# Other costs and a tiling charge in the list scheduler of a six-layer transformer kernel

## What is computed

```python
for i in range(DEPTH):                      # 4 layers, kinds 0, 1, 2, 0
    ...                                     # x @ w_in, rope on q and k
    mix = dsa_attention / dilated_attention / moba_attention
    mo = memory_attention(qm, mk, mv)       # 4 heads over 256 memory rows
    x = layer_norm(ALPHA * x + concat(mix, mo) @ w_out[i])
    x = layer_norm(ALPHA * x + swiglu(x, w_gate_up[i], w_down[i]))
for l in range(DEPTH_2):                    # 2 layers
    ...                                     # h = rms_norm(x), u = h @ w_in[l]
    oa = diff_attention(...)                # 4 heads, two maps each
    ob = mla_attention(...)                 # 8 heads of width 64 + 32
    oc = sliding_window_attention(...)      # 8 heads with sinks
    y = gates0 * (oa @ w_br_a) + gates1 * (ob @ w_br_b) + gates2 * (oc @ w_br_c)
    x = x + rms_norm(y @ w_out)
    x = x + sigmoid(x @ w_ple_gate) * (p @ w_ple_proj)
```

## Time and profile before

| | |
|---|---|
| median of 3 runs | 1916.89 us (1916.48 to 1917.0) |
| profiled execution, its time | 1914.78 us |
| profiled execution, its span | 1912.9 us |
| TensorE busy | 1866.8 us, 98% |
| GpSimd busy | 1520.1 us, 79% |
| ScalarE busy | 938.1 us, 49% |
| VectorE busy | 813.0 us, 42% |

### The profile page before, as it was taken

One profiled execution on the slowest core, in us unless ns is written; L12 is line 12 of the kernel. 1 busy time (PEld: TensorE's weight loads), 2 busy tenths in 40 slices (PEclk: granted clock), 3 DMA queues, 4 the chain that ended last, 5 costly groups with the idle time before them and its releaser, 6 DMA issues.

```text
span 1912.9 us, 27394 instructions
## 1 busy us (share of the span) xinstructions
PE 1866.8 (98%) x9610; PEld 1528.5 (80%) x9610; DVE 813.0 (42%) x1944; ACT 938.1 (49%) x1485; POOL 1520.1 (79%) x1330
## 2 busy tenths in 40 slices
PE   7999999999999999999999999999999999999998
PEld 6778888877888887788888678887787887788877
DVE  7884110446311155411147741106747445446534
ACT  4554444454544345444435644434656644555752
POOL 7758989885897977797987679797786887777785
PEclk9999999999999999999999999999999999999999
DMA  8444656564776554465655446655564564556453
GB/s 285 127 151 152 189 153 234 182 190 111 202 199 209 183 180 149 140 187 154 234 157 153 162 157 186 196 191 169 174 181 129 156 203 162 163 175 178 131 168 107
DMA packets 184557, 330.54 MB, mean 173 GB/s; under 512 B 12220, under 2 KB 44520, under 8 KB 184424
## 3 DMA queue, kind: packets, MB, share of 16 engines
q1 hardware_dynamic: 176512, 323.21, 54.6%
q10 hardware_dynamic: 7912, 5.59, 1.0%
HBM read 325.35 MB, written 3.41 MB: 172 GB/s over the span
## 4 chain that ended last, share of the span: by engine, by line
PE 85%; DVE 6%; POOL 5%; DMA 1%; issue 1%; ACT 1%; ACTq 0%; DVEq 0%
PE acc L1412 24%; PE acc L1413 23%; PE acc L1419 21%; POOL w_lo L1182 5%; PE tps L1359 4%; PE acc L1434 3%; PE acc L1415 2%; PE ops L1476 2%; PE tps L1452 2%; DMA raw<-in_w_down 1%; PE acc L1383 1%; PE acc L1385 1%; PE acc L1384 1%; PE ops L1371 1%; DMA L<-in_positions 0%
## 5 line engine op out<-in xcount | busy, mean ns | idle before, releaser
L1182 POOL TENSOR_TENSOR w_lo<-raw,w_hi 128x512 fp32r<-128x512 f32 (+2 forms) x1242 | 1479.2, 1228 | 346.8 <-ACT w_hi L1210 345.7
L1210 ACT CAST w_hi<-raw 128x1024 fp32r<-128x1024 f32 (+3 forms) x624 | 615.5, 992 | 746.7 <-PE acc L1419 567.4
L1412 PE MATMUL acc<-w_hi,xT_hi 128*128 128x512 f32 (+1 forms) x1808 | 687.4, 384 | 13.5 <-POOL w_lo L1182 3.6
L1413 PE MATMUL acc<-w_lo,xT_hi 128*128 128x512 f32 (+1 forms) x1808 | 666.4, 372 | 0.0
L1419 PE MATMUL acc<-w_hi,xT_lo 128*128 128x512 f32 (+2 forms) x1744 | 505.1, 371 | 0.5 <-DVE xT_lo L1689 0.5
L1412 PEld LDWEIGHTS acc<-w_hi,xT_hi 128*128 128x128 f32 x1808 | 341.3, 189 | 86.6 <-issue 22.2
L1413 PEld LDWEIGHTS acc<-w_lo,xT_hi 128*128 128x128 f32 x1808 | 342.1, 189 | 51.9
L1419 PEld LDWEIGHTS acc<-w_hi,xT_lo 128*128 128x128 f32 x1744 | 317.6, 189 | 58.6 <-DVE xT_lo L1689 1.6
L1749 DVE TENSOR_TENSOR H<-G,acc 128x512 f32<-128x512 f32 (+1 forms) x48 | 30.9, 644 | 334.5 <-PE acc L1419 334.5
L1412 PE MATMUL acc<-w_hi,hT_hi 128*128 128x512 f32 x352 | 139.6, 397 | 2.9 <-POOL w_lo L1182 2.5
L1413 PE MATMUL acc<-w_lo,hT_hi 128*128 128x512 f32 x352 | 137.3, 390 | 0.0
(11 more groups left out here) (208 smaller groups left out, 2000.7 us busy)
## 6 DMA issues: line engine op xcount, KB each, us to landing
raw<-in_w_gate_up SPq DMA_DIRECT2D x160, 512.0 KB, 3.8
raw<-in_w_in SPq DMA_DIRECT2D x104, 512.0 KB, 3.9
raw<-in_w_down SPq DMA_DIRECT2D x88, 512.0 KB, 3.9
raw<-in_w_out SPq DMA_DIRECT2D x48, 512.0 KB, 3.5
raw<-in_w_in_a SPq DMA_DIRECT2D x32, 512.0 KB, 3.8
raw<-in_w_in_b SPq DMA_DIRECT2D x20, 512.0 KB, 4.6
raw<-in_w_mem_kv SPq DMA_DIRECT2D x16, 512.0 KB, 4.2
raw<-in_w_gate_up SPq DMA_DIRECT2D x32, 256.0 KB, 2.8
```

Of the source, the lines that this page charges most:

```text
L1182: ins = nc.gpsimd.tensor_tensor(w_lo[:, r, i, 0:ch.width], raw[:, r, i, 0:ch.width], w_hi[:, slot, i, 0:ch.width].bitcast(F32), ALU.subtract)
L1210: nc.scalar.copy(w_hi[:, u.u % SPLIT, 0:u.nk, 0:u.chunk.width], raw[:, u.u % RAW, 0:u.nk, 0:u.chunk.width]).then_inc(S["hi_ready"], 1)
L1412: nc.tensor.matmul(o, hi[:, tok], wh, start=first_k, stop=False)
L1413: ins = nc.tensor.matmul(o, hi[:, tok], wl, start=False, stop=False)
```

## The change

The list scheduler gets a notion of tiling. Scores, values and index tasks count as tiled, all other tasks of TensorE do not. If TensorE's last task was tiled, any task that isn't can begin only 250 ns (LEAVE) after its clock; a tiled task that follows another kind ends 90 ns later (ENTER). The cost of scores goes from 450 ns for each map to 100 + 0.33 for each column of all maps, that of values from 800 to 350 ns. The code that emits instructions is not changed; their order and the PSUM banks that tasks get come from the list.

```diff
--- before.py
+++ after.py
@@ -47,6 +47,7 @@
 SPLIT = 8
 LAG = 5
 CROSS = 120
+ENTER, LEAVE = 90, 250
 FIRST_CONSTANTS = 3
 CONSTANTS = 8
 REL_CONSTANTS = 3
@@ -341,12 +342,19 @@
                     best = (at, slots)
             return best
 
+        def tiled(k):
+
+            return k.kind in ("scores", "values", "index")
+
+        mode = False
         left = len(self.tasks)
         while left:
             first = None
             for e, tasks in ready.items():
                 for k in tasks:
                     at = max(k.at, clock[e])
+                    if e == "PE" and mode and not tiled(k):
+                        at = max(at, clock[e] + LEAVE)
                     if k.room is not None:
                         where = place(k)
                         if where is None:
@@ -366,7 +374,11 @@
                     rooms[k.room[0]][b] = k
             k.begin = first[0][0]
             k.end = k.begin + k.cost
+            if k.eng == "PE" and tiled(k) and not mode:
+                k.end += ENTER
             clock[k.eng] = k.end
+            if k.eng == "PE":
+                mode = tiled(k)
             if k.sem is not None:
                 count[k.sem] = count.get(k.sem, 0) + k.inc
                 k.n = count[k.sem]
@@ -500,7 +512,7 @@
             s.qk = qk[i] if isinstance(qk, dict) else qk
             b1, b3 = s.before, s.before3
             wide = s.width * s.maps
-            s.scores = self.task("PE", "scores", s, 450 * s.maps, "scores_ready",
+            s.scores = self.task("PE", "scores", s, 100 + 0.33 * wide, "scores_ready",
                                  [*s.qk, *s.apart, b1.scores if i else None], prio=0,
                                  room=("acc", s.banks or score_banks))
             after = [s.scores, s.mask_at]
@@ -529,7 +541,7 @@
                 s.take[j] = self.task("DVE", "take_turn", (s, j), 160 + 1.03 * P * blocks, "t_taken",
                                       [s.turn[j], b1.values if b1 is not None else None], prio=0)
                 s.turn[j].release = s.take[j]
-            s.values = self.task("PE", "values", s, 800, "pv_ready", [*s.take[:s.turns], *s.fed], prio=0,
+            s.values = self.task("PE", "values", s, 350, "pv_ready", [*s.take[:s.turns], *s.fed], prio=0,
                                  room=("ops", [(0,), (1,)]))
             if s.flipped:
                 ready = s.values
```

## The result

The changed kernel takes 1925.15 us (median of 7 runs, 1921.67 to 1931.78), the kernel before beside it 1917.0 us (1914.58 to 1918.95). The ratio is 1.0041, with a 95% interval of 1.0026 to 1.0055: slower by some 8 us. Lines of the code stand 12 further down: products are L1424, L1425, L1427 and L1431, scores L1446, transposes of probabilities L1464, values L1488.

A forecast was written before the change was run, and what follows sets the result against it. TensorE was taken as the bound. From the profiled 1914.78 us, merges took 1.2, wrongly tiled tasks and waits 0, giving 1913.6; the median lies 2.1 higher, so 1915.7 us, with an 8-in-10 range of 1905 to 1926.

The forecast's parts named there:

- The bound and where to look: TensorE sets the end; only the six stretches with attention, idle 22.4 us together, can change much.
- The merges: Tiled tasks becoming neighbours in TensorE's order: four at 0.14 us and three at 0.21, together 1.2 us saved.
- The wait term: All TensorE waits together, moved by the new order: taken as 0, bounds -8.5 and +10 us.
- the thin cover: End of layer 3's attention: no next layer's memory products there; TensorE waits 1.11 us for VectorE's low part.
- The rival of the late chain: Planner's clock runs short, splits and evictions queue, uncovered tails end later: 1920.7 or 1925.7 us; chance 0.25.
- Fewer waits: Rival: short costs put more products between scores and transposes, so the softmax is ready: about 1909 us; chance 0.35.
- The wrong set of tiled tasks: Latent scores and differential values, 8 + 8 tasks, charged as tiled although they are not: 0, bound 4 us.
- What moves with it: Transposes behind scores come 0.8 us later, with VectorE's copy, values, ScalarE's output and w_out products; costs nothing where covered.
- The clock: TensorE's granted clock in the stretches, read as 0.99 or 1.00 of full speed; no term for it.
- The feed-forward stretches: They hold no tiled task; a difference there would contradict the whole picture.

The follow-up runs named there:

- lengths in layer 3 alone: The changed kernel with measured lengths of scores and values for layer 3's steps only, other stretches keeping their order: 1920.34 us, 1.0023 to before.
- measured lengths: The changed kernel with scores and values costs as the rows give them: 1917.85 us; with latent scores and differential values also not counted as tiled, 1915.42 us.

## Why the prediction failed, step by step

**The bound and where to look: right.** TensorE sets the end, and the six stretches are 8.5 us longer where the whole span grew by 8.9 (the start gives 1.7 back, the feed-forward stretches take 2.0); 6.3 us of them are idle time, beyond the 4 us that the prediction named as the point at which it is wrong. The median, 1925.15, lies near the end of its range of 1905 to 1926, on the other side of before than the forecast of 1915.7.

**The merges: right in count and size.** I counted the changes into a tiled form in the trace: 99 before, 92 after (four fewer in layer 0, one in layer 1, four in layer 3, one more in each LW). Values and scores as neighbours take 0.80 us, 0.81 in the earlier trace rows:

```profile
123.86 0.88 PE L1488 MATMUL ops<-PT,U 128*64 128x256 f32 x8
124.66 0.93 PE L1446 MATMUL acc<-KT,QT 64*128 64x128 f32 x8
125.52 0.87 PE L1464 MATMUL tps<-ident,L 128*128 128x128 f32 x6
```

In layers 0 and 3 drift less added idle time (sum of the gaps between modelled ends: 2.3 - 2.5 and 1.4 - 1.8) leaves some -0.3 us each for eight entries: with layer 1 (0.8 - 1.2) about -1.0 for nine, where the sum has -1.2 us. It is too small to matter.

**The wait term: taken as 0, measured at some +6 us, and this is the step that failed.** The sum 1914.78 - 1.2 puts all waits together at 0; the six stretches have 6.3 us more of them. The prediction gave bounds of -8.5 and +10 and chose between them without a row for it. The rows at hand, layer 3's tail and the thin cover, stood on the side of a loss. The rival of the late chain named the places, layer 0, layer 3 and the differential stretches, and all but the first differential one paid, with 0.8 us in layer 1 as well. Its mechanism was half right, and in layer 3 alone. There the planner's short clock did it, as lengths in layer 3 alone show (3.3 us of drift). In layer 0 it did not: measured lengths leave 2.0 of its 2.3 us. And no split or eviction came late: in the six stretches TensorE waits for no low half, before or after, and its waits for ScalarE's U (L1240, now L1252) fell from 3.0 to 1.4 us. What happened in layer 3 is simpler: the list believes scores and values to be cheap and TensorE to be free early, puts them and the transposes close together, and spends on them no products, so that values stand directly behind their transposes. That the list does this because of its short clock is argued from its rule; the rows show the order, and that it goes with the short lengths. "Fewer waits" argued the opposite from the same short clock, that products would be spent more freely, and was wrong.

**The wrong set of tiled tasks: priced at 0 with a bound of 4, measured at 3 us** (1.0008 against 0.9991). The cover I named, that TensorE runs behind the plan, answers for idle time in the plan; but the charges change which task comes first, and that order is kept on the chip. With the change's short lengths the wrong set was not tried by itself.

**What moves with it: one move was missed.** VectorE's `latent_scale` came late, directly ahead of `sub_gate` and into GpSimd's low halves: 2.2 us of wait, 2.3 of drift. The prediction spoke of the copies, not of tasks of VectorE that have nothing to do with scores, and nowhere of GpSimd holding VectorE, although before shows it, for instance at 16.59 us above.

**The clock: not in the sum.** The prediction read 0.99 and 1.00 and went on. A wait of 1.9 or 2.2 us costs 1.7 us more if the clock falls behind it. Before and change have two falls each ahead of the end in their profiled executions, so most of it cancels: the change's two cost 1.7 each, before's 1.7 at the start and some 0.4 in differential 1, which leaves 1.3 of the 8.9 us. In the medians it has a share. Each run has a mean granted clock, and one fall takes 0.0009 off it (half of 3.4 us in 1922). Three runs of the change at 0.998 average 1923.9 us, sixteen of before at 0.998 1917.2 us: 6.8 us at the same clock. All seven runs of the change average 0.9971, 65 of before 0.9980, about one fall more, which fits five long waits against two. So of the 8 us some 7 are the order's waits and the rest, by this estimate, the clock; seven runs are few for it.

**The feed-forward stretches** differ after all: 2.0 us in "all the rest", of which 1.5 lie just behind layer 3, where one load of w_down took 7.93 us from issue to landing instead of 6.34. The kernels with the same order there show between 0.0 and 1.5 us, so this is the execution's, not the order's; the sentence that such a difference would contradict the picture was too strong.

Still open is layer 0: 2.3 us in every kernel with the change's costs there, of which before's own costs give back all and measured lengths 0.3. The waits seen are a sum of small ones (U, L1640, 2.7 instead of 2.0 us; scores for KT 1.1; L of GpSimd 0.6), and no run takes them one by one.

## What to carry to other kernels

In this kernel the order that the list scheduler makes is a draw: without falls the orders tried lie 1.0 to some 4 us apart in each stretch, and costs nearer to the rows gave the better one in some stretches and the worse one in others, while the effect that is modelled (0.40 us for an entry) is worth 1 us in all. So build several orders, read each stretch by the drift of the same products, and put the best ones together; that gave 9 us where no single set of costs gave over 1.6. And look at what stands in an engine's queue ahead of the task for which the busiest engine waits: small instructions there may be long ones at that time.

## What was not expected of the hardware

Some of VectorE's instructions on SBUF alone are held while GpSimd's `tensor_tensor` runs: one of 0.16 us takes 1.2 beside pieces of 512 columns, one of 0.19 us takes 0.67 beside 256, none is held beside 32 (0 of 1944 instructions over 0.4 us). In before the excess is at most 1.1 us, in 33 instructions of 1944; some 1480 overlap GpSimd, so most are not held. But beside an unbroken row of pieces of 256 columns one instruction was held for 11.1 us. The Trainium skill (Advanced Engine Details and Errata, GPSIMD Details) says that the Pool engine shares a read and a write interface with DVE and conflicts with DVE instructions that have two SBUF inputs, or are in a 2-port mode. The rows agree as to the partner: of the 33 in before, 29 are `scalar_tensor_tensor` or `tensor_tensor`. The other four are `tensor_scalar` with one SBUF input, as at 16.59 us; whether these were in a 2-port mode no run here shows. The rows add the size: as long as one GpSimd instruction in most cases, and a whole row of them in two.

The granted clock falls to 0.50, the 1.2 GHz level, mostly for 3.4 us at a time, behind about half of TensorE's waits of 1.9 to 3.1 us (21 of 43), twice behind two waits of 0.8 or 0.9 us close together, and three times within longer waits. It costs 1.7 us where TensorE is the bound. An execution has 0 to 4 falls ahead of its end, and the same order has them in one execution and not in another.
